# Two heads per score product, no zero products, and norm sums placed inside the chunks of a two-layer block

## Chip, cores, metric

One core of one Trainium2 chip runs the whole program. The metric is device time in microseconds of one execution; three executions of the kernel before and a profiled one are given.

## What is computed

Two layers over 512 positions of width 1024. Each layer has a mixer and a convolutional feed-forward part, both between norms:

```python
h = rms_norm(x, mix_pre_g) * (1 + scale_m) + shift_m
q, k, v, x_lru, gate = split(h @ w_in)               # 512, 128, 128, 512, 512 columns
# chunks of 64 queries see 128 keys; 8 query heads of 64 share 2 key heads; a sink joins the softmax
attn = sliding_window_attention(rope(q), rope(k), v, sinks)
lru = rg_lru(causal_dwconv(x_lru)) * gelu(gate)
y = concat(rms_norm(attn, g_attn), rms_norm(lru, g_lru)) @ w_out
x = x + gate_m * rms_norm(y, mix_post_g)
h = rms_norm(x, ffn_pre_g) * (1 + scale_f) + shift_f
g, val = split(causal_dwconv(h @ w_up))              # 3072 columns each
x = x + gate_f * rms_norm((gelu(g) * val) @ w_down, ffn_post_g)
```

`scale`, `shift` and `gate` are products of silu(c) with `ada_w`, 4 MB for each of twelve vectors. Everything is float32.

## The kernel before

Everything lies transposed: 128 rows of the width on the partitions, positions on the free side, so `x` and `y` are eight tiles of 128x512. Each weight chunk (512 KB, 128 output columns) is split into a high part (ScalarE copy to fp32r, L567) and a low part (VectorE subtraction, L1111); so is each activation (`hH`, `hL`, or `mH`, `mL`). One output tile is 8 x 3 products: high by high, high by low, low by high. A ring of six chunk slots is refilled by SyncE once TensorE has used a chunk. Every engine has its own hand-written order of steps; semaphores tie them.

At a transition a norm must be finished before the next product can start. So the positions are cut in two halves `h` of 256: while TensorE works on half 1 of the last chunks of one matrix, the norm of half 0 goes on, and while it works on half 0 of the next matrix (`next_group`), the norm of half 1 does. `k = 0` is the transition from `w_out` to `w_up`, `k = 1` the one from `w_down` to the `w_in` of the next layer. A norm chain of one half goes so: squares (ScalarE), their sum over tiles (VectorE, `add_square`), the sum over partitions (TensorE, products of one column with `ones`, `post_sums_mm`), root (ScalarE, `post_root`), reciprocal (VectorE, `post_recip`), spread over partitions (TensorE, `post_spread`), residual update (VectorE, `x_update`), squares of the new `x` (`x_squares`), `x_fold`, `x_sums_mm`, `x_root`, `x_recip`, `x_spread`, and then per tile `tmp_half`, `hi_half`, `lo_half` make the operands of the next products.

Two chunks share one PSUM bank of 512 columns, a half each (`pair_bank`). Before their products, `open_bank` writes the bank with a product of zeros (`nil`) that has 512 columns. Scores of a pair of windows (`scores_mm`) are 16 products of 64 rows by 64 stationary columns, for each of 8 heads and of two windows one. During layer 0, VectorE also makes the `ada_w` dot products (`mod_unit`, L1117, called by `late` at the transition), whose weights GpSimd fetches.

## Time and profile before

| | us |
|---|---|
| median of 3 executions | 1204.27 (1202.68 to 1209.97) |
| profiled execution, its own time | 1212.97 |
| span in its trace | 1211.2 |
| TensorE busy | 1176.0 |
| VectorE busy | 833.5 |
| ScalarE busy | 540.4 |
| mean granted TensorE clock | 0.972 |

Busy time is a union of instruction spans. Matmuls overlap in the pipeline, so what one costs is read from start to start, not from its length. An fp32 product shows as two records, an fp32r product as one.

### The profile page before, as it was taken

The numbers are of one execution on the slowest core, as the hardware profiler recorded it, in microseconds if no ns is written. First come the engines' busy times: TensorE is split into PE (matmuls) and PEld (weight loads), VectorE is DVE, ScalarE is ACT, GpSimd is POOL, SyncE is SP. The second block draws the span as 40 slices with busy tenths as digits, with TensorE's granted clock in tenths as the row PEclk, the third lists the DMA queues.
The fourth block names the chain that finished last, engine by engine and source line by source line (L and its number), as shares of the span: only waits on it lengthen the run. The fifth ranks groups of instructions, "written<-read, shape, count | busy, mean of one in ns | idle before, by whom it ended". The sixth has DMA issues, their size and how long they took to land.

```text
span 1211.2 us, 16364 instructions
## 1 busy us (share of the span) xinstructions
PE 1176.0 (97%) x6686; PEld 1024.2 (85%) x6686; DVE 833.5 (69%) x1307; ACT 540.4 (45%) x880; POOL 53.4 (4%) x110
## 2 busy tenths in 40 slices
PE   7999998999999999999999999999999999999995
PEld 6986898988788888888999779998888888888895
DVE  8899858788877777677587874477753565356645
ACT  5387725454224431444348874445532444134430
POOL 4000010001110011000000000000000000000000
PEclk8999888999999999999999999989999999999997
DMA  9833435046784458544113220304233332323312
GB/s 358 338 105 106 157 103 177 7 169 209 229 275 141 141 187 288 178 143 139 53 36 106 70 85 21 105 1 139 89 103 93 98 102 90 105 88 103 92 48 70
DMA packets 44940, 155.81 MB, mean 129 GB/s; under 512 B 5056, under 2 KB 7360, under 8 KB 44864
## 3 DMA queue, kind: packets, MB, share of 16 engines
q1 hardware_dynamic: 34352, 116.48, 29.2%
q0 software_dynamic: 10368, 37.75, 9.4%
q8 instruction: 53, 0.87, 0.3%
q10 hardware_dynamic: 144, 0.52, 0.1%
q14 instruction: 23, 0.19, 0.0%
HBM read 152.64 MB, written 2.10 MB: 128 GB/s over the span
## 4 chain that ended last, share of the span: by engine, by line
PE 80%; DVE 11%; ACT 5%; issue 2%; DMA 2%; SPq 1%; DVEq 0%
PE ps L1841 80%; DVE sb_wL L1111 2%; DVE sb_R L1572 1%; DVE sb_y L1174 1%; DMA sb_raw<-in_w 1%; DMA sb_stage<-in_ada 1%; ACT sb_R L794 1%; DVE sb_R L1700 1%; DVE sb_x L1178 1%; DVE sb_R L1697 1%; ACT sb_wH L567 1%; PE ps L2087 1%; DVE sb_y L1196 1%; ACT sb_sq L673 0%; DVE sb_adaw L1117 0%
## 5 line engine op out<-in xcount | busy, mean ns | idle before, releaser
L1841 PE MATMUL ps<-sb_hH,sb_wH 128*128 128x512 f32 (+1 forms) x1184 | 422.6, 363 | 6.5 <-ACT sb_hH L614 4.0
L1841 PE MATMUL ps<-sb_hH,sb_wL 128*128 128x512 f32 (+1 forms) x1184 | 417.7, 358 | 0.0
L1841 PE MATMUL ps<-sb_hL,sb_wH 128*128 128x512 f32 (+1 forms) x1184 | 394.9, 358 | 2.3 <-DVE sb_hL L1203 2.3
L1841 PEld LDWEIGHTS ps<-sb_hH,sb_wH 128*128 128x128 f32 x1184 | 228.6, 193 | 42.1 <-ACT sb_hH L614 5.4
L1841 PEld LDWEIGHTS ps<-sb_hH,sb_wL 128*128 128x128 f32 x1184 | 228.5, 193 | 31.4
L1841 PEld LDWEIGHTS ps<-sb_hL,sb_wH 128*128 128x128 f32 x1184 | 214.1, 192 | 34.9 <-DVE sb_hL L1203 2.9
L567 ACT ACTIVATE sb_wH<-sb_raw 128x1024 fp32r<-128x1024 f32 x174 | 181.1, 1052 | 129.4 <-DMA sb_raw<-in_w 129.3
L1111 DVE TENSOR_TENSOR sb_wL<-sb_raw,sb_wH 128x1024 fp32r<-128x1024 f32 x174 | 211.4, 1219 | 30.0 <-ACT sb_wH L567 29.8
L1841 PE MATMUL ps<-sb_mH,sb_wH 128*128 128x256 f32 (+1 forms) x608 | 206.4, 340 | 0.6 <-ACT sb_mH L1019 0.6
L1841 PE MATMUL ps<-sb_mL,sb_wH 128*128 128x256 f32 (+1 forms) x608 | 205.0, 337 | 0.0
L1841 PE MATMUL ps<-sb_mH,sb_wL 128*128 128x256 f32 (+1 forms) x608 | 204.9, 337 | 0.0
L1697 DVE SCALAR_TENSOR_TENSOR sb_R<-ps,sb_par,sb_R 128x511 f32<-128x511 f32 x84 | 62.9, 749 | 98.9 <-ACT sb_R L1013 98.9
L1841 PEld LDWEIGHTS ps<-sb_mH,sb_wH 128*128 128x128 f32 x608 | 118.0, 194 | 12.4 <-ACT sb_mH L1019 1.1
L1841 PEld LDWEIGHTS ps<-sb_mL,sb_wH 128*128 128x128 f32 x608 | 117.9, 194 | 12.3 <-DVE sb_mL L1709 0.4
L1841 PEld LDWEIGHTS ps<-sb_mH,sb_wL 128*128 128x128 f32 x608 | 117.7, 194 | 11.1
L1013 ACT ACTIVATE sb_R<-ps,sb_par 128x512 f32<-128x512 f32 x84 | 65.2, 776 | 112.3 <-PE ps L1841 112.3
L1019 ACT ACTIVATE sb_mH<-sb_I 128x512 fp32r<-128x512 f32 x42 | 26.5, 632 | 101.1 <-DVE sb_I L1707 101.1
L1700 DVE SCALAR_TENSOR_TENSOR sb_R<-ps,sb_par,sb_R 128x510 f32<-128x510 f32 x84 | 62.9, 749 | 3.0
L1117 DVE SCALAR_TENSOR_TENSOR sb_adaw<-sb_adaw,sb_csb 128x1024 f32<-128x1024 f32 x44 | 53.4, 1220 | 8.2 <-DMA sb_adaw<-in_ada 8.0
L1709 DVE TENSOR_TENSOR sb_mL<-sb_I,sb_mH 128x512 fp32r<-128x512 f32 x42 | 29.1, 693 | 29.3 <-ACT sb_mH L1019 29.3
L1009 ACT ACTIVATE sb_I<-sb_R 128x512 f32<-128x512 f32 x42 | 26.6, 633 | 50.0 <-DVE sb_R L1700 50.0
L614 ACT ACTIVATE sb_hH<-sb_y,sb_mod 128x256 fp32r<-128x256 f32 x48 | 22.8, 502 | 29.5 <-DVE sb_y L1196 29.4
(229 smaller groups left out, 1154.2 us busy)
## 6 DMA issues: line engine op xcount, KB each, us to landing
sb_raw<-in_w SPq DMA_DIRECT2D x174, 512.0 KB, 3.6
sb_adaw<-in_ada POOLq DMA_DIRECT2D x44, 512.0 KB, 4.8
sb_stage<-in_ada SPq DMA_DIRECT2D x24, 512.0 KB, 14.2
sb_vw<-in_ada POOLq DMA_DIRECT2D x22, 512.0 KB, 4.7
sb_side<-in_w SPq DMA_DIRECT2D x8, 512.0 KB, 5.0
sb_raw<-in_w SPq DMA_DIRECT2D x8, 384.0 KB, 14.8
sb_stage<-in_ada POOLq DMA_DIRECT2D x6, 512.0 KB, 4.6
sb_x<-in_x SPq DMA_DIRECT2D x4, 512.0 KB, 5.8
```

Source lines behind the costliest of these rows:

```text
L567: nc.scalar.activation(high_of(n), raw_of(n), ACT.Copy).then_inc(w_hi, 1)
L614: nc.scalar.activation(hH[:, j, part_of(h)], yt(j)[:, part_of(h)], ACT.Identity, bias=bias[:, j:j + 1], scale=1.0).then_inc(hi_ready, 1)
L794: last = nc.scalar.activation(R[:, c % 4, part_of(h)], pair_bank(h, p)[:, (c % 2) * HALF:(c % 2 + 1) * HALF], ACT.Identity, bias=pcol(l, " ...
L1009: nc.scalar.activation(I[:, p % 2, :], R[:, (c - 1) % 4, :], ACT.Gelu_apprx_tanh).then_inc(f_gelu, 1)
L1013: nc.scalar.activation(R[:, c % 4, :], bank(up_bank(u)), ACT.Identity, bias=par_l[:, COLS["fcb"] + col:COLS["fcb"] + col + 1], scale=pcol( ...
L1019: nc.scalar.activation(mH[:, p, :], I[:, 2 + p % 2, :], ACT.Copy).then_inc(act_hi, 1)
L1111: TT(low_of(n), raw_of(n), high_of(n).bitcast(fp32), ALU.subtract).then_inc(w_lo, 1)
L1117: STT(out=tile, in0=tile, scalar=1.0, in1=csb[:, :], op0=ALU.mult, op1=ALU.mult, accum_out=mod[:, seg, kt:kt + 1]).then_inc(ada_used, 1)
L1697: link(STT(out=buf[:, 1:], in0=acc[:, 0:SEQ - 1], scalar=pcol(l, "fcw", 2 * PAIRS + col), in1=buf[:, 1:], op0=ALU.mult, op1=ALU.add))
L1700: STT(out=buf[:, 2:], in0=acc[:, 0:SEQ - 2], scalar=pcol(l, "fcw", col), in1=buf[:, 2:], op0=ALU.mult, op1=ALU.add).then_inc(f_taps, 1)
L1709: TT(mL[:, p, :], I[:, 2 + p % 2, :], mH[:, p, :].bitcast(fp32), ALU.subtract).then_inc(act_lo, 1)
L1841: return nc.tensor.matmul(out, a, b, start=start, stop=stop, **kw)
```

## The change

Four things are altered.

- Scores: `q` is stored so that two heads of a window lie side by side (`turned`), and `scores_mm` makes 8 products of 64 rows by 128 stationary columns, key head 0 and 1 in turn, each key head in a bank of its own. The rows of a score tile are then two heads of 64 queries instead of two windows.
- Zeros: `open_bank` is gone; the first product into a bank carries the start flag.
- Norms: the last squares of a half are no longer added on VectorE but summed over partitions by products of their own (`post_final`), after the sum of the others (`post_early`); at `k = 0` the epsilon comes in as one product with `ident`, and `post_variance` goes. `x_sums_mm` is split in `x_early` and `x_final`. The gate factor is applied by ScalarE as it copies `y` out of PSUM, one instruction per tile; `x_update` at `k = 0` is then one multiplication of 1024 columns instead of four of 256. The calls stand at new places in every engine's order: at `k = 0` `x_final` and `x_spread` of half 0 stand between the products of the last two chunks of `w_out`.
- Around it: seven slots instead of five hold `ada_w` units at this point (five of them in turn instead of three), and the first chunk after the group of six is split before `pair_base(1, 0)` and `pair_taps(1, 0)` instead of behind them.

```diff
-        ADDS = [6, 5]
+        ADDS = [4, 3]
+        def score_tile(half, kv, two):
+            return kv * AT + half * (AT // 2) + two
+        def two_heads(two, w):
+            first = two * 2 * SEQ + w * P
+            return y[:, first:first + P]
...
                 def out_evict(h, i):
+                    if h == 0 and i == 0:
+                        act.wait_ge(fac_ready, l + 1)
...
-                        square(l, 0, 3 * h + i - 1, pair_bank(h, i))
-                    nc.scalar.activation(y4[:, 2 * i:2 * i + 2, part_of(h)],
-                                         pair_bank(h, i).rearrange("p (j t) -> p j t", j=2),
-                                         ACT.Copy).then_inc(out_copied, 1)
+                        nc.scalar.activation(last_sq[h], pair_bank(h, i), ACT.Square).then_inc(last_ready, 1)
+                    for c in range(2):
+                        j = 2 * i + c
+                        last = nc.scalar.activation(yt(j)[:, part_of(h)],
+                                                    pair_bank(h, i)[:, c * HALF:(c + 1) * HALF],
+                                                    ACT.Copy, scale=fac[:, l, 1, j:j + 1])
+                    last.then_inc(out_copied, 1)
...
                 for p in range(3):
+                    if p == 0:
+                        split_step(ring_next(U0 + 1, SLOTS_W - 1))
                     pair_base(1, p)
                     for c in range(2 * p, 2 * p + 2):
-                        if c:
+                        if c > 1:
                             split_step(ring_next(U0 + c, SLOTS_W - 1))
...
-                for j in range(4 * q, 4 * q + 4):
-                    V.mark(STT(out=yt(j)[:, part_of(h)], in0=yt(j)[:, part_of(h)], scalar=fac[:, l, 2 * k + 1, j:j + 1],
-                               in1=bank(POST_BANK[h])[:, 0:HALF], op0=ALU.mult, op1=ALU.mult))
+                if k == 0:
+                    V.mark(TT(ys, ys, rb.unsqueeze(1).broadcast_to([P, 4, HALF]), ALU.mult))
...
                 U0 = B + FFN0
                 factors(l, 1)
                 late(8, 2)
+                late(10, 1)
                 add_square(l, 0, 0, 0)
-                late(10, 2)
+                late(11, 2)
                 add_square(l, 0, 1, 0)
-                late(12, 1)
-                add_square(l, 0, 2, 0)
                 dve.sem_inc(post_summed, 1)
-                late(13, 1)
-                post_variance(l, 0)
+                late(13, 3)
                 post_recip(l, 0, 0)
                 x_update(l, 0, 0, 0)
                 x_update(l, 0, 0, 1)
+                factors(l, 2)
                 x_fold(l, 0, 0, 0)
                 lo_chunk(U0)
                 x_fold(l, 0, 0, 1)
-                late(14, 2)
...
-            def post_sums_mm(l, k, h):
+            def post_early(l, k, h):
                 pe.wait_ge(post_summed, norm_half(l, k, h))
-                half_sums(h, 0, sum_of[h]).then_inc(post_cols, 1)
+                if k == 0:
+                    part_mm(bank(STAT_BANK[h])[:, 0:2], ident[:, :], eps_a[:, 2 * h:2 * h + 2], True, False)
+                half_sums(h, 0, sum_of[h], k == 1, False)
+                if k == 1:
+                    for t in range(2):
+                        first = h * HALF + t * P
+                        part_mm(bank(STAT_BANK[h])[:, t:t + 1], sum_full[:, first:first + P], ones[:, 0:1],
+                                False, False)
+            def post_final(l, k, h):
+                pe.wait_ge(last_ready, norm_half(l, k, h))
+                half_sums(h, 0, last_sq[h], False, True).then_inc(post_cols, 1)
...
-                    for s in range(NQ):
-                        at_ = HD * (s // AT)
-                        for half in range(2):
-                            w = (2 * t + half) * CHUNK
-                            last = mm(bank(0, 2)[half * CHUNK:(half + 1) * CHUNK, s * P:(s + 1) * P],
-                                      yt(s % AT)[at_:at_ + HD, w:w + CHUNK],
-                                      kd[at_:at_ + HD, w:w + P], True, True)
+                    for half in range(2):
+                        w = (2 * t + half) * CHUNK
+                        for two in range(AT // 2):
+                            for kv in range(NKV):
+                                at_, s = HD * kv, score_tile(half, kv, two)
+                                last = mm(bank(0, 2)[:, s * P:(s + 1) * P],
+                                          two_heads(two, 2 * t + half)[at_:at_ + HD, :],
+                                          kd[at_:at_ + HD, w:w + P], True, True)
...
                 for h in range(2):
+                    if h:
+                        post_early(l, 0, 0)
                     for c in range(GRP):
...
+                        split = KT - 1 if h and c == 1 else AT
+                        if split > AT:
+                            half_products(acc, n, h, mH, mL, range(AT, split), False, False)
+                            post_spread(l, 0, 0)
...
+                        if h and c == 0:
+                            post_final(l, 0, 0)
+                        if h and c == GRP - 1:
+                            x_early(l, 0, 0)
...
-                x_sums_mm(l, 0, 0)
-                x_spread(l, 0, 0)
                 def statistics(k):
...
-                        if at_ == 1:
-                            post_sums_mm(l, k, 1)
-                        if at_ == 3:
+                        if at_ == 0:
+                            post_early(l, k, 1)
+                        if at_ == 2 * KT + GRP + 1:
+                            post_final(l, k, 1)
+                        if at_ == 2 * KT + GRP + 2:
                             post_spread(l, k, 1)
+                        if at_ == (KT + GRP + 4 if k == 0 else KT + 4):
+                            x_early(l, k, 1)
                         if at_ == KT + 4:
-                            x_sums_mm(l, k, 1)
+                            x_final(l, k, 1)
```

## Rows read from the trace of the kernel before

**Rows 1.** Page: busy time by engine, and the granted TensorE clock in 40 slices.
```profile
PE 1176.0 (97%) x6686; PEld 1024.2 (85%) x6686; DVE 833.5 (69%) x1307; ACT 540.4 (45%) x880; POOL 53.4 (4%) x110
...
PEclk8999888999999999999999999989999999999997
```

**Rows 2.** Groups of TensorE instructions by line and form, whole run (count | busy, mean | idle).
```profile
L1841 PE MATMUL ps<-sb_nil 128*128 128x512 f32 x36 | 13.8, 463 | 1.1 <-ACT sb_adaw L742 1.1
```

**Rows 3.** Timeline of TensorE, layer 0, scores of the second window pair (start, length).
```profile
88.47 1.59 PE L1841 MATMUL ps<-sb_kd,sb_y 64*64 64x128 f32 x32
90.00 1.98 PE L1841 MATMUL ps<-sb_xc,sb_gw 128*128 128x512 f32 x4
92.64 1.09 PE L2087 MATMUL ps<-sb_ident,sb_work 128*128 128x128 f32 x8 [0.66 <-DVE sb_work L1331]
```

**Rows 4.** Timeline of TensorE, layer 0, from w_out to w_up, first half.
```profile
185.04 0.95 PE L1841 MATMUL ps<-sb_ones,sb_ssqv 128*128 128x1 f32 x8
...
197.87 1.84 PE L1841 MATMUL ps<-sb_ones,sb_R 128*128 128x1 f32 x16
200.33 0.71 PE L1841 MATMUL ps<-sb_ident,sb_tiny 128*128 128x128 f32 x4 [0.62 <-DVE sb_tiny L1189]
...
204.65 0.58 PE L1841 MATMUL ps<-sb_hH,sb_wH 128*128 128x256 f32 x1 [2.89 <-ACT sb_hH L614]
```

**Rows 5.** Timeline of TensorE, layer 0, second half of the same transition.
```profile
222.59 1.95 PE L1841 MATMUL ps<-sb_ones,sb_R 128*128 128x1 f32 x16 [0.37 <-DVE sb_R L1183]
...
226.67 1.05 PE L1841 MATMUL ps<-sb_ident,sb_tiny 128*128 128x128 f32 x4
...
229.32 0.60 PE L1841 MATMUL ps<-sb_nil 128*128 128x512 f32 x2
229.76 0.28 PE L1841 MATMUL ps<-sb_hH,sb_wH 128*128 128x256 f32 x1
...
249.45 0.50 PE L1841 MATMUL ps<-sb_hH,sb_wH 128*128 128x512 f32 x1 [1.27 <-DVE sb_wL L1111]
```

**Rows 6.** Timeline of TensorE, layer 1, the same three places.
```profile
769.81 0.95 PE L1841 MATMUL ps<-sb_ones,sb_ssqv 128*128 128x1 f32 x8
...
810.25 1.06 PE L1841 MATMUL ps<-sb_ident,sb_tiny 128*128 128x128 f32 x4
...
832.90 0.50 PE L1841 MATMUL ps<-sb_hH,sb_wH 128*128 128x512 f32 x1 [1.13 <-DVE sb_wL L1111]
```

**Rows 7.** Groups of VectorE instructions by form, 166 to 262 us.
```profile
L1111 DVE TENSOR_TENSOR sb_wL<-sb_raw,sb_wH 128x1024 fp32r<-128x1024 f32 x11 | 13.0, 1217 | 0.0
...
L1174 DVE SCALAR_TENSOR_TENSOR sb_y<-sb_y,sb_fac,ps 128x256 f32<-128x256 f32 x16 | 6.6, 476 | 2.1 <-PE ps L1841 2.1
...
L1178 DVE TENSOR_TENSOR sb_x<-sb_x,sb_y 128x1024 f32<-128x1024 f32 x4 | 4.9, 1225 | 0.1
```

**Rows 8.** Groups of ScalarE instructions by form, 166 to 262 us.
```profile
L567 ACT ACTIVATE sb_wH<-sb_raw 128x1024 fp32r<-128x1024 f32 x11 | 11.2, 1050 | 0.0
L614 ACT ACTIVATE sb_hH<-sb_y,sb_mod 128x256 fp32r<-128x256 f32 x16 | 7.7, 502 | 11.1 <-DVE sb_y L1196 11.1
...
L783 ACT ACTIVATE sb_y<-ps 128x512 f32<-128x512 f32 x8 | 4.7, 591 | 0.0
```

**Rows 9.** Stretches at the lower clock: busy time, and the granted clock third from last.
```profile
143.00:160.00 17.00, 17.00 (x79) 16.82 (x79) 6.70 (x14) 4.93 (x11) 1.62 (x4) 0.50 0.31 103
...
224.90:228.30 3.40, 3.40 (x18) 3.40 (x18) 0.67 (x3) 0.02 (x1) 0.00 (x0) 0.51 0.02 5
```

**Rows 10.** Timeline of TensorE from w_down of layer 0 to w_in of layer 1.
```profile
632.35 1.95 PE L1841 MATMUL ps<-sb_ones,sb_R 128*128 128x1 f32 x16 [0.37 <-DVE sb_R L1183]
...
649.41 0.39 PE L1841 MATMUL ps<-sb_hL,sb_wH 128*128 128x256 f32 x1 [0.86 <-DVE sb_hL L1203]
```

**Rows 11.** Timeline of TensorE: end of the first up group, and the tail.
```profile
309.54 0.50 PE L1841 MATMUL ps<-sb_mH,sb_wH 128*128 128x512 f32 x1 [0.63 <-ACT sb_mH L1019]
...
1198.41 1.86 PE L1841 MATMUL ps<-sb_ones,sb_scr 128*128 128x1 f32 x8 [2.75 <-DVEq L1744]
```

More of the change, by code:

```diff
@@ L272, in build @@
         stage_in = [sem(f"stage_in{i}") for i in range(2 * KT)]
-        ada_in = [sem(f"ada_in{i}") for i in range(5)]
+        ada_in = [sem(f"ada_in{i}") for i in range(7)]
         ada_used = sem("ada_used")
@@ L357, in rope_no, with turned @@
             return l * GRP + h * (GRP // 2) + i + 1
+        def score_tile(half, kv, two):
[3 more added lines that the diff above has]
+            return y[:, first:first + P]
+        def turned(j, n, h):
+            first = j // 2 * 2 * SEQ + h * SEQ + j % 2 * CHUNK
+            step = 2 * SEQ - CHUNK if j % 2 else CHUNK
+            if n == 1:
+                rows = y[:, first:first + SEQ].rearrange("p (w m q) -> p w m q", w=4, m=2)
+                return rows[:, :, 0, :]
+            rows = y[:, first:first + n * step].rearrange("p (j r) -> p j r", j=n)[:, :, 0:SEQ]
+            return rows.rearrange("p j (w m q) -> p j w m q", w=4, m=2)[:, :, :, 0, :]
         def in_bank(i):
@@ L403, in build @@
         LATE_UNITS = range(IN_UNITS.stop, DEPTH * NMOD * KT)
+        OUT_UNITS = range(IN_UNITS.stop, 5 * KT)
         def unit_slot(u):
-            return u % 2 if u in IN_UNITS else 2 + u % 3
+            if u in IN_UNITS:
+                return u % 2
+            return 2 + ((u - OUT_UNITS.start) % 5 if u in OUT_UNITS else (u - OUT_UNITS.stop) % 3)
         def unit_fill(u):
@@ L1640, in _ @@
                 lo_half(l, 0, 0, 3)
-                post_variance(l, 1)
                 lo_half(l, 0, 0, 4)
@@ L1947, in next_group @@
                         finish(last, h, c)
+                        between(h, KT + c)
                     for c in range(4, GRP):
@@ L1968, in half_sums @@
                         first = g * HALF + t * P
-                        last = mm(bank(STAT_BANK[h])[:, at_ + t:at_ + t + 1], src[:, first:first + P], ones[:, 0:1],
-                                  g == 0, g == 1)
+                        last = part_mm(bank(STAT_BANK[h])[:, at_ + t:at_ + t + 1], src[:, first:first + P], ones[:, 0:1],
+                                       opens and t == 0 and g == 0, closes and g == 1)
                 return last
@@ L2031, in _ @@
                     mm(pair_bank(h, i), nil[:, :], nil[:, 0:1].broadcast_to([P, SEQ]), True, True)
-            for h in range(2):
-                for i in range(GRP // 2):
-                    open_bank(h, i)
             pe.wait_ge(csb_ready, 1)
@@ L2338, in _ @@
                             pe.wait_ge(dn_read, dn_no(l, GROUPS - 1, 1))
[L2339 to L2349 removed]
+                        acc, n = pair_acc(h, i, c), D0 + c
+                        split = KT // 2 + 1 if h and c == 2 else KT // 2
+                        if h and c == 2:
+                            post_early(l, 1, 0)
+                        half_products(acc, n, h, mH, mL, range(split), True, False)
+                        if h and c == 2:
+                            post_final(l, 1, 0)
+                        if h and c == 6 and l + 1 < DEPTH:
+                            x_early(l, 1, 0)
+                        if h and c == 7 and l + 1 < DEPTH:
+                            x_spread(l, 1, 0)
+                        last = half_products(acc, n, h, mH, mL, range(split, KT), False, True)
+                        finish(last, h, c)
+                        if h and c == 2:
+                            post_spread(l, 1, 0)
+                        if h and c == 6 and l + 1 < DEPTH:
+                            x_final(l, 1, 0)
                 if l + 1 < DEPTH:
@@ L2352, in _ @@
                 else:
-                    post_sums_mm(l, 1, 1)
+                    post_early(l, 1, 1)
+                    post_final(l, 1, 1)
                     post_spread(l, 1, 1)
@@ L2428 @@
     put("fcw", columns(a["ffn_conv_w"].reshape(L, FCONV * 2 * DFF)))
-    put("sink", np.broadcast_to(a["attn_sinks"][:, None, :], (L, P, NQ)))
+    row_head = np.array([[kv * AT + 2 * two + p // CHUNK for kv in range(NKV) for _ in range(2) for two in range(AT // 2)]
+                         for p in range(P)])
+    put("sink", a["attn_sinks"][:, row_head])
     half = HD // 2
```

212 lines of the change are left out of this document (104 added, 108 removed).

## The prediction

> **What bounds the kernel now.** The page comes first: TensorE is busy for 1176.0 of 1211.2 us, at full clock in most slices [rows 1]. So the end is set by TensorE's own work, by its few gaps, and by the stretches in which it is granted half of its 2.4 GHz. The windows show the last: 17 us from 143 on, 3.4 us from 224.9 on, and five more like these [rows 9]. The timeline of TensorE then shows the gaps in the places that the change touches. In layer 0, after the last product of `w_out`, come 16 column sums, 0.62 us idle, the spread, the zero products, and 2.89 us idle until `hH` is there [rows 4]; in the second half 0.37 us idle before the sums and 1.27 us before the first chunk of 512 columns [rows 5]. Each time the clock fell after such a place: TensorE had done 16 one-column sums and waited. Layer 1 repeats the places [rows 6], the transition to `w_in` has two of them [rows 10].
>
> Prices are taken from start to start. Two zero products take 229.76 - 229.32 = 0.44 us, 0.22 each [rows 5]. From 185.04 to 197.87 stand 96 products of 256 columns, eight records of column sums (0.95) and a spread: 12.83 us, so with 0.12 for a product 0.36 are left for the spread [rows 4]. Sixteen records of column sums take 1.84 [rows 4], 0.115 each.
>
> **Scores.** Now 32 records from 88.47 to 90.00 [rows 3], 1.53 us. A record streams 128 columns and still starts 0.048 after the one before, less than half of the 0.109 below, so several run at once; the two windows of a head use different columns of the array, the key heads different rows. After the change there are 16 records in two row groups, each key head's eight in a row. Eight records one after the other take eight times 0.109 (the 0.12 of 256 columns, less a little), 0.9 us with its start about 1.0: a gain of 0.5 per call. If the row groups don't run at once, it is 16 x 0.109 = 1.75, a loss of 0.2. I take the gain, since two groups of columns share the array in the row shown. Of eight calls two stand ahead of 92.64, where TensorE waits 0.66 for `normalise` on VectorE anyway [rows 3]: nothing. Six give 3.0 us. The Trainium skill (TensorEngine Tiling, Theoretical Speedup) lets products that are small both ways run up to four at once, those that are small one way two; by that rule the 32 records would need eight steps before and the 16 need eight after, and nothing would be gained. The row disagrees for before: 1.53 us are 14 steps of 0.109, not eight.
>
> **Zeros.** 36 records of such products of 512 columns are in the trace [rows 2], 30 go. Six at the start lie before a wait; twelve are in `next_group` and counted below. Of twelve in `attn_products` most cost 0.22, those in the 17 us at half clock [rows 9] twice that; two in layer 0 stand ahead of small waits. Together 12 x 0.22 + 0.4 - 0.4 = 2.6 us.
>
> **`w_out` to `w_up`, the main term.** I count from the start of half 1 of `w_out` to the start of the last spread (`x_spread` of half 1). Before: the post sums start two chunks of 12 products (2.88) after it, and the last spread at 226.67, so 226.67 - 185.04 + 2.88 = 44.5 us [rows 4, 5]. Layer 1: 810.25 - 769.81 + 2.88 = 43.3 [rows 6]. After, if TensorE never waits and the clock stays up: 120 + 132 = 252 products x 0.12 = 30.2; column sums in half 0 34 records (two of the epsilon product, 8 + 8, 8 + 8) and in half 1 as many, 68 x 0.115 = 7.8; three spreads 1.1. That is 39.1 us: 5.4 and 4.2 less. The change adds column sums here (20 records, 2.3 us, since what VectorE no longer adds is summed by products) and takes away 3.5 us of gap, 0.9 of zeros, 0.4 of waiting and the two low-clock stretches.
>
> Does TensorE never wait? VectorE and ScalarE have to keep step. From start to start an instruction costs some 0.08 us less than its length on VectorE and 0.1 less on ScalarE; so a low part of a chunk 1.14, a step of 256 columns (`tmp`, `lo`) 0.4 [rows 7], a high part 0.95, `hi` 0.41 [rows 8]. `x_update` was 4 x 0.41 + 1.14; now it is twice the 1.14 of a 1024-column addition, 2.3 instead of 2.8 [rows 7]. An eviction on ScalarE was 2 x 0.49; the copy becomes two of 256 columns at 0.41 to 0.46 [rows 8], so 1.4 instead of 1.0, which is 0.4 more, 16 times, on an engine that is idle half the time here. Counting the new order through from the start of half 1: post spread at 4.6; `x_update` done at 7.6 and 9.9 (layer 0's last three `ada_w` units end at about -0.4, since five slots keep them fetched); second `x_fold` at 12.5, wanted at 13.5; `hi_half` 0 at 17.9, wanted at 19.1; low part of chunk 3 at 18.8, wanted at 19.1; in the next half post reciprocal at 24.1, wanted at 25.0; second fold at 33.9, wanted at 36.8. Everything fits, with margins of 0.3 to 3 us. That is thin: what is late next is VectorE.
>
> Behind the last spread, the chunk of 512 columns started 249.45 - 226.67 = 22.8 us later [rows 5], in layer 1 22.65 [rows 6]. TensorE's own work is 0.36 + 13 x 1.44 = 19.1. The split of that chunk moves ahead of four tap operations, 2.2 us earlier, and `lo_half` 7 ahead of `pair_taps(0, 1)`; so about 20.1, a gain of 2.6. Layer 1 keeps it: 4.2 + 2.6 = 6.8. Layer 0 doesn't: there VectorE, with its `ada_w` units, is behind TensorE for the whole first up group, and TensorE waits for it at 309.54 [rows 11]. What TensorE gains over VectorE is lost there; VectorE's own gain is that of the spread, 5.4 + 0.3 at full clock, less 0.5 for taps that now stand behind the split: 5.2. Price if that were wrong: up to 2.4 more.
>
> **`w_down` to `w_in`.** Half 0 gets 12 more records (8 + 4 + 8 instead of 8), 1.34 us, and so does half 1; two pairs of zeros (0.88), the wait ahead of 632.35 (0.4 shown, 0.8 with the drain) and the low clock behind it (0.8 within the stretch) go; but the wait at 649.41 grows by 0.6, because it is `lo_half` 7 on VectorE that ends it [rows 10]. Sum 2.7 - 0.9 - 0.8 - 0.8 - 0.4 + 0.6, near 0; between -1.5 and +2.
>
> **Tail.** Half 0 of the last layer gets 1.3 us of column sums; the last sums, for which TensorE waits 2.75 us [rows 11], no longer wait for two additions on VectorE of 512 and 256 columns, 1.2 by the prices above: -1.2. Near 0.
>
> **Sum.** -3.0 - 2.6 - 5.2 - 6.8 = -17.6 against 1212.97. The median of the runs is 8.7 us lower than the profiled execution, as if some of the low-clock stretches were not in it (17 us at half clock alone cost up to 8.5 [rows 9]). About 3 us of my sum are such stretches; I take half off. Thin margins and new column sums will cost some stalls; 2 us for them. 1204.3 - 17.6 + 1.5 + 2 = 1190.2.
>
> **Rivals.** (1) The chain on VectorE and ScalarE becomes the bound inside the chunks: the gap moves between products, where TensorE's order makes it wait at `post_final`, `post_spread` or `lo_half`. For it: margins of 0.3 us, 0.4 us more per eviction, VectorE behind in layer 0. Against it: VectorE does 3 us less per layer. Half of the 12 us is lost: 1196.5. (2) The row groups don't overlap: 6 x 0.7 = 4.3 more, 1194.5. (3) The slower side: the clock. Column sums keep TensorE occupied but are not the work that holds its clock up [rows 5, 9]; the change has more of them, and the zero products of 512 columns, which were work to the clock, are gone. If it falls after each of eleven groups of sums, each costs 1.7 us (3.4 at half speed), and if layer 1's attention norm, where it fell for 3.4 us, gets a stretch like the 17 us of layer 0, 7 more: 1190 + 19 + 7 = 1216, slower than before from about eight falls on. Against it: after the change 12 products stand between two groups of eight records, where 16 stood in a row. The Trainium skill has this rule (TensorE: Matmul & The Clock Gate, The HAM clock gate): throttled is the default state and activity releases it; by it removing idle time pays twice, and removing products of zeros can cost. (4) The moved pieces gain only what the zeros and scores do: 1204.3 - 5 = 1199.
>
> **Chances.** Forecast 1190 (own range 1185 to 1195) 0.55; rival 1 0.24; rival 2 0.09; rival 3 0.05; rival 4 0.07. About 1% (12 us) is what a measurement of this kernel can tell from no change; below 1192.2 counts as faster. Nearly all of that lies in the forecast's case, two thirds of it and a deeper tail: faster 0.50, within 1% 0.45, slower 0.05. The range has to reach rival 1 and most of 4, and downward a case where layer 0 keeps its 2.4 and the low-clock stretches weigh in full: 1183 to 1200.
>
> **What would show it.** Scores: 16 records in about 1.0 us; 1.75 is rival 2. Only six records with `nil` and 512 columns. From the first `post_early` of a layer to the last `x_spread` about 39 us, with no idle time over 0.5 us on TensorE and no slice of PEclk below 9 there; idle time ahead of a product that reads `hL`, or of a spread, is rival 1; lower clock behind column sums is rival 3. In layer 0 the wait near 309.54 grows from 0.6 to about 3 us. The first up chunk of 512 columns starts about 20 us after the last spread. The prediction is wrong if layer 0's first up group ends as late as before, or if 17 us at half clock come and go between executions and hide the rest.

## Result and profile after

The changed kernel takes 1198.51 us (median of 11 runs, 1192.47 to 1201.18); the kernel before, run beside it, 1204.27 (11 runs, 1201.89 to 1212.32). The ratio of the two is 0.9941, with a 95% interval of 0.992 to 0.9961. By the ratio the change gives 7.1 us, 0.6%; by the two medians it gives 5.8. The direction is as forecast, but 14.1 us were forecast (1204.3 - 1190.2), so the gain is half of it by the ratio and two fifths by the medians. The two profiled executions are further apart, 1212.97 and 1199.15 us, with spans of 1211.2 and 1197.3.

The page of the changed kernel, busy times and granted clock (before: [rows 1]):

```profile
PE 1165.3 (97%) x6616; PEld 1016.3 (85%) x6616; DVE 821.9 (69%) x1267; ACT 544.4 (45%) x896; POOL 52.1 (4%) x110
...
PEclk8999889999999999999999999999999999999998
```

TensorE lost 10.7 us of busy time. In the clock line each digit stands for 30 us. Only the slices from 120 to 180 us and the two ends are low; the low slices of the transitions before are gone.

Zero products and scores, groups by form and the timeline of TensorE in layer 0 (before: [rows 2, 3]):

```profile
L1869 PE MATMUL ps<-sb_nil 128*128 128x512 f32 x6 | 1.6, 395 | 0.0
```

```profile
110.98 1.16 PE L1869 MATMUL ps<-sb_kd,sb_y 64*128 64x128 f32 x16
112.07 1.09 PE L1869 MATMUL ps<-sb_adaw,sb_vw 128*64 128x256 f32 x8
```

Six zero products are left. The 16 score records take 1.09 us where the 32 took 1.53.

From `w_out` to `w_up` in layer 0, timeline of TensorE (before: [rows 4, 5]):

```profile
180.30 0.28 PE L1994 MATMUL ps<-sb_tiny,sb_ident 128*128 128x2 f32 x2
180.44 1.03 PE L1994 MATMUL ps<-sb_ones,sb_ssqv 128*128 128x1 f32 x8
...
184.81 0.60 PE L1869 MATMUL ps<-sb_ident,sb_tiny 128*128 128x128 f32 x4
...
196.01 0.60 PE L1869 MATMUL ps<-sb_ident,sb_tiny 128*128 128x128 f32 x4
...
219.37 0.60 PE L1869 MATMUL ps<-sb_ident,sb_tiny 128*128 128x128 f32 x4
...
240.31 0.50 PE L1869 MATMUL ps<-sb_hH,sb_wH 128*128 128x512 f32 x1 [1.63 <-DVE sb_wL L1149]
...
248.27 0.50 PE L1869 MATMUL ps<-sb_hH,sb_wH 128*128 128x512 f32 x1 [2.20 <-DVE sb_wL L1149]
```

Within this stretch TensorE no longer waits for a column sum or a spread. The first post sum now stands at the start of half 1 of `w_out`, and from there to the last spread it is 219.37 - 180.30 = 39.1 us, where 44.5 stood. But 20.9 us further on TensorE waits for the low part of the first chunk of 512 columns, and again for the second; layer 1 has the same two waits (1.51 at 815.95, 2.22 at 823.91). In the view of TensorE's waits (total, times, longest) this is now the largest item; it was 2.4 us in two waits before (1.27 of it in [rows 5], 1.13 in [rows 6]):

```profile
PE ps L1869 <- DVE sb_wL L1149: 7.6, 4, 2.2
PE ps L1869 <- DVE sb_tiny L1251: 5.4, 1, 5.4
PE ps L1869 <- DVE sb_ssqv L1269: 3.5, 1, 3.5
PE ps L2129 <- DVE sb_mL L1429: 1.5, 1, 1.5
```

The windows of the changed kernel (length; busy time of TensorE, its weight loads, VectorE, ScalarE, GpSimd; then the granted clock as a share of 2.4 GHz) show where the clock is low (before: [rows 9]):

```profile
138.50:159.00 20.50, 20.35 (x94) 19.23 (x95) 8.73 (x17) 6.15 (x14) 3.14 (x6) 0.50 0.41 145
180.44:221.24 40.80, 40.80 (x349) 40.80 (x348) 28.56 (x44) 21.21 (x39) 0.00 (x0) 1.00 0.27 89
240.31:253.85 13.54, 11.33 (x48) 9.04 (x49) 11.01 (x31) 7.70 (x13) 0.00 (x0) 1.00 0.32 107
824.50:827.90 3.40, 3.40 (x10) 2.62 (x9) 2.40 (x8) 2.54 (x5) 0.00 (x0) 0.51 0.02 8
```

In this trace the transition of layer 0, column sums included, runs at 1.00. The attention half of layer 0's `w_out` has 20.5 us at 0.50, the lower of the two levels (1.2 GHz). In layer 1 another 3.4 us at the lower level follow right behind the second of the two waits, at 824.50.

### The profile page after: what moved, and what is told of

Read it like the earlier page. It is cut to its first block, busy times and chain, and to the rows that moved or that the text cites. A ratio compares the mean times of both kernels' runs of the same rounds, so it can differ in the third digit from the quotient of the medians.

```text
span 1197.3 us, 16181 instructions
## 1 busy us (share of the span) xinstructions
PE 1165.3 (97%) x6616; PEld 1016.3 (85%) x6616; DVE 821.9 (69%) x1267; ACT 544.4 (45%) x896; POOL 52.1 (4%) x110
## 4 chain that ended last, share of the span: by engine, by line
PE 80%; DVE 13%; ACT 4%; issue 2%; DMA 1%; SPq 0%; DVEq 0%
PE ps L1869 57%; PE ps L1894 21%; PE ps L1994 2%; DVE sb_wL L1149 2%; DVE sb_R L1614 1%; DVE sb_stage L1155 1%; ACT sb_R L828 1%; ACT sb_wH L595 1%; DVE sb_R L1736 1%; DVE sb_R L1733 1%; DVE sb_y L1233 1%; ACT sb_sq L700 1%; DVE sb_xc L1381 0%; DVE sb_adaw L1155 0%; DMA sb_raw<-in_w 0%
## 5 line engine op out<-in xcount | busy, mean ns | idle before, releaser
L1869 PE MATMUL ps<-sb_hH,sb_wH 128*128 128x512 f32 x800 | 315.3, 394 | 7.6 <-DVE sb_wL L1149 7.6
L1869 PE MATMUL ps<-sb_hH,sb_wL 128*128 128x512 f32 x800 | 312.1, 390 | 0.0
L1869 PE MATMUL ps<-sb_hL,sb_wH 128*128 128x512 f32 x800 | 311.9, 390 | 0.0
L1149 DVE TENSOR_TENSOR sb_wL<-sb_raw,sb_wH 128x1024 fp32r<-128x1024 f32 x174 | 211.7, 1219 | 30.3 <-ACT sb_wH L595 30.1
L1869 PE MATMUL ps<-sb_mH,sb_wH 128*128 128x512 f32 x288 | 112.1, 389 | 0.9 <-ACT sb_mH L1055 0.9
L1869 PE MATMUL ps<-sb_mL,sb_wH 128*128 128x512 f32 x288 | 112.2, 389 | 0.0
L1869 PE MATMUL ps<-sb_mH,sb_wL 128*128 128x512 f32 x288 | 112.1, 389 | 0.0
L1894 PE MATMUL ps<-sb_hH,sb_wH 128*128 128x256 f32 x384 | 104.3, 290 | 0.1
L1894 PE MATMUL ps<-sb_hH,sb_wL 128*128 128x256 f32 x384 | 102.9, 287 | 0.0
L1894 PE MATMUL ps<-sb_mH,sb_wH 128*128 128x256 f32 x320 | 94.6, 296 | 0.2 <-ACT sb_adaw L769 0.2
L1894 PE MATMUL ps<-sb_mL,sb_wH 128*128 128x256 f32 x320 | 92.4, 289 | 0.0
```

Of the source, the lines that this page charges most:

```text
L1149: TT(low_of(n), raw_of(n), high_of(n).bitcast(fp32), ALU.subtract).then_inc(w_lo, 1)
L1869: return nc.tensor.matmul(out, a, b, start=start, stop=stop, **kw)
L1894: return nc.tensor.matmul(out, a, b, start=start, stop=stop, skip_group_check=True)
```

## Where the time went: a ledger by stages

Each stage runs from the first product of one kind to the first of the next, so that the same stage of the program stands in each row (us). P is what the prediction gave the stage. The last three columns come from experiments 8 and 7 below: the two kernels with twelve products of zeros added in the stage of the second row, layer 0, which held the clock there.

| stage | before | after | diff. | P | before, clock held | after, clock held | diff. |
|---|---|---|---|---|---|---|---|
| start to layer 0's `w_out` | 131.65 | 128.04 | -3.6 | -1.0 | 132.91 | 127.89 | -5.0 |
| attention half of `w_out`, to the spread | 30.14 | 32.02 | +1.9 | -1.3 | 24.19 | 23.77 | -0.4 |
| from there to the end of the first up group | 147.75 | 143.11 | -4.6 | -5.2 | 147.75 | 144.65 | -3.1 |
| up and down groups, transition to `w_in` | 350.01 | 349.57 | -0.4 | 0 | 349.38 | 351.07 | +1.7 |
| layer 1: `w_in`, scores | 63.09 | 61.61 | -1.5 | -2.0 | 63.09 | 61.61 | -1.5 |
| attention half of `w_out` | 23.92 | 21.55 | -2.4 | -1.3 | 22.40 | 21.55 | -0.9 |
| from there to the end of the first up group | 145.67 | 143.46 | -2.2 | -6.8 | 145.61 | 141.87 | -3.7 |
| the rest | 318.93 | 317.98 | -1.0 | 0 | 317.61 | 317.48 | -0.1 |
| span | 1211.2 | 1197.3 | -13.8 | -17.6 | 1202.9 | 1189.9 | -13.1 |

The second row went against the forecast by 3.2 us, and the seventh, layer 1's transition, fell short by 4.6. The trace of the changed kernel with zeros has 3.4 us at the lower clock in the third and in the fourth row which the changed kernel's own trace doesn't have; they cost 1.5 us each. It lacks the 3.4 us at 824.50 in the seventh, where it is 1.6 us shorter.

The clock enters this ledger in two places, and the traces of all kernels together show both (numbers in brackets are those of the experiments). "Wait" is TensorE's wait ahead of the transposition of layer 0's last probabilities, which lies in the stage of the second row. "Low in stage" is the time at the lower clock in that stage, and "low elsewhere" the same for the rest of the program, without the first 30 us and the last 20.

| trace | scores | norms | wait | stage | low in stage | low elsewhere |
|---|---|---|---|---|---|---|
| before, first | old | old | 0.28 | 30.1 | 17 | 27 |
| before, again (1) | old | old | none | 24.7 | 6 | 20 |
| norms alone (3) | old | new | none | 24.6 | 6 | 7 |
| zeros alone (4) | old | old | 0.71 | 21.9 | 0 | 24 |
| scores alone (5) | new | old | 1.10 | 30.9 | 17 | 24 |
| scores and zeros (2) | new | old | 1.54 | 32.1 | 21 | 20 |
| changed | new | new | 1.53 | 32.0 | 21 | 3 |
| changed, split back (9) | new | new | 1.54 | 28.7 | 14 | 10 |
| changed, base ahead (10) | new | new | 1.53 | 32.0 | 21 | 3 |
| changed, attention zeros back (6) | new | new | 1.10 | 24.7 | 3 | 7 |
| changed, twelve zeros (7) | new | new | 0.21 | 23.8 | 0 | 7 |
| the same and base ahead (11) | new | new | 0.22 | 23.8 | 0 | 3 |
| the same and second split (12) | new | new | 0.22 | 23.8 | 0 | 3 |
| before, twelve zeros (8) | old | old | none | 24.2 | 0 | 20 |

The column on the right goes by the norms: 20 to 27 us at the lower clock with the old ones, 3 to 10 with the new. The column beside it goes more by the scores: with the new ones and no zeros added or put back it is 14 to 21 us in all five traces, and with the old ones and no zeros added it is 17, 6, 6 and 0. The wait alone doesn't decide it, since the first trace has 17 us behind a wait of 0.28.

## Experiments

All times are medians, with the ratio to runs of the kernel before on the same chip and its 95% interval. The experiments were run on three chips, on which the kernel before has medians of 1203.46 to 1204.50 us. Each run also has its mean granted clock. The runs of one kernel lie near a line, 8 to 11 us for 0.01 of clock where the clock varies much; "at 0.982" is the value of that line. It compares kernels at the same mean clock and says nothing of where the low clock lies; where no run of a kernel reached 0.982, as in experiments 2 and 5, it is an estimate from outside its runs.

**1. The kernel before again.** No edit.

> The kernel before, unchanged, for the granted clock of each of its runs. Eleven runs of the changed kernel lie on one line: 1192.47 us at a granted clock of 0.990, 1196.7 to 1198.5 at 0.984, 1201.2 at 0.980, so 8.7 us for 0.01 of clock. Theory A: the profiled execution of the kernel before (1212.97 us at 0.972) carried low-clock stretches that most of its executions lack; on the same slope 1204.3 us lies at 0.982, and at equal clock the two kernels are 5 to 7 us apart, half of the 13.8 us between the two profiled executions. Theory B: at equal clock they are 10 us or more apart, and the change itself lowers the clock (stretch of 20.5 us at half clock in layer 0); then most runs of before show a clock of 0.986 or more at 1204 us.

1205.00 us, ratio 1.001 (0.998 to 1.004); clocks 0.972 to 0.986, median 0.980. In the 35 runs of the kernel before beside it the same: 1199.84 to 1213.14 us, median 0.980, 1202.7 us at 0.982. The changed kernel has 1198.9 at 0.982 and a median clock of 0.984. So neither theory quite: 3.8 us at equal clock, and over the whole program the change raises the mean clock rather than lowering it. The profiled execution of the kernel before, at 0.972, was at the low end of its runs. The second trace has, in the attention half of layer 0's `w_out`:

```profile
133.34:158.02 24.68, 24.35 (x181) 23.59 (x180) 17.69 (x34) 14.76 (x24) 2.09 (x4) 0.87 0.29 102
```

24.7 us at a mean clock of 0.87, where the first trace had 30.1. This stage is 5.5 of the 6.8 us between the two.

**2. and 3. The two halves of the change.** In one kernel scores and zeros as after and the norms as before, in the other the reverse: the hunks of `turned`, `score_tile`, `two_heads`, `scores_mm`, `outputs_mm` and the sinks, and those of the zeros, of which the core is

```diff
-                    if c % 2 == 0:
-                        open_bank(h, c // 2)
-                    half_products(pair_acc(h, c // 2, c), O0 + c, h, mH, mL, range(AT), False, False)
+                    half_products(pair_acc(h, c // 2, c), O0 + c, h, mH, mL, range(AT), c % 2 == 0, False)
```

> The kernel before with the new scores and without the zero products, norms as before. Prediction's own terms: scores 3.0 and zeros 2.6 us (zeros of the transitions 1.8 more, as far as they are not ahead of a wait), so 1198 us. Theory A: most of this lies ahead of waits or behind a longer low-clock stretch in layer 0's attention norm (the trace of the changed kernel is only 0.8 us ahead when w_out's second half starts); 1201 to 1203. Rival 4 (only these two gain anything): 1198 to 1199, and the run with the norms alone is at 1204.

1204.76 us, ratio 1.0002 (0.9977 to 1.0026). Above what either theory said: no gain, at clocks of 0.969 to 0.976 where before has 0.972 to 0.986. At 0.982 the line gives 1198.7, 4.1 less. By this estimate the clock took back what the products gave.

> The changed kernel with the scores of before and with the zero products put back: the norm chains inside the chunks, the seven slots and the earlier split alone. Prediction: 12 us less than before in work and short low-clock stretches, so 1193 us. Theory A: 4 us in layer 0 and 3 in layer 1, some of it short low-clock stretches that most runs of before lack: 1199 to 1201. Rival 4: 1204, no gain.

1201.08 us, ratio 0.9975 (0.9949 to 1.0), clock 0.986. Between the prediction and nothing, as theory A had it. At 0.982 its line gives 1205.7 us, 3.0 more than the kernel before. So the norms' gain shows as a higher clock (0.986 at the median for 0.980), in line with the 7 us at the lower clock where the old norms have 20 to 27; at equal clock they cost time. By their ratios the two halves alone add up to 2.8 us, and together they give 7.1. Each of these ratios is uncertain by some 3 us, so it isn't shown that the halves depend on each other.

**4. and 5. Zeros alone, scores alone,** on the kernel before: the same hunks, each group by itself.

> The kernel before without its zero products, nothing else. Scores and zeros together gave no time (1204.8) at a median clock of 0.974 instead of 0.980, and 4.1 us less at equal clock. Theory Z (the zeros carry the clock): this run shows clocks of 0.972 to 0.976 and 1203 to 1206 us. Theory S (the shorter scores do): clocks as before, 0.980, and 1201 to 1202.

1201.39 us, ratio 0.9985 (0.996 to 1.0011). Seven runs at 1199.6 to 1201.4 us and 0.979 to 0.982, five at 1208.4 to 1208.9 and 0.972 to 0.974. The traced execution is one of the seven and has no low clock in the attention half of layer 0; that the other five have the stretch there is inferred from their clock, as no trace of them was kept. The median clock stays at 0.980 and the median time is in theory S's range, so the zeros alone don't carry the clock.

> The kernel before with the new scores, zeros kept. 16 records take 1.09 us instead of 1.53, so eight calls give up to 3.5 us of work. Theory Z: clocks as before and 1200.5 to 1202. Theory S: clocks of 0.972 to 0.976 and 1203 to 1206. Phase (neither alone, the clock falls by where the small steps happen to lie): something between, and different in each.

1205.14 us, ratio 1.0003 (0.9982 to 1.0024), clocks 0.975 to 0.980 in all twelve runs. The shorter scores alone gain nothing and never have the good executions of the kernel before. Theory S is nearer. A likely reason stands where layer 0's last probabilities are transposed. Timelines of TensorE: the changed kernel, scores alone, norms alone (where scores are as before):

```profile
136.47 1.06 PE L2129 MATMUL ps<-sb_ident,sb_adaw 128*128 128x128 f32 x8 [1.53 <-DVE sb_mL L1429]
137.37 0.95 PE L1869 MATMUL ps<-sb_ones,sb_sq 128*128 128x1 f32 x8
138.65 1.98 PE L1869 MATMUL ps<-sb_adaw,sb_vw 128*64 128x256 f32 x8 [0.33 <-ACT sb_adaw L779]
140.56 1.87 PE L1869 MATMUL ps<-sb_ones,sb_I 128*128 128x1 f32 x8
```

```profile
136.13 1.06 PE L2112 MATMUL ps<-sb_ident,sb_adaw 128*128 128x128 f32 x8 [1.10 <-DVE sb_mL L1411]
```

```profile
139.36 1.04 PE L2109 MATMUL ps<-sb_ident,sb_adaw 128*128 128x128 f32 x8
```

With the scores of before TensorE is here at 139.4 and doesn't wait (0.28 us in the first trace of the kernel before). With the new ones it starts 3 us earlier and waits 1.1 us, with the zeros gone too 1.5, for VectorE's softmax and low parts. What it gained ahead of this place partly ends in the wait. Behind the wait come only transpositions, column sums and small outputs, and from 138.50 on the clock is 0.50 for 20.5 us. The Trainium skill (TensorE: Matmul & The Clock Gate, HAM oscillation) tells of a kernel whose TensorE waits for transfers between its groups of products and is throttled again each time. Here the wait is for VectorE and short, 1.53 us. The trace agrees in the order only, a wait and then the fall, and the small products around the wait didn't prevent it. The wait is not the whole cause: the first trace of the kernel before fell at the same place with 0.28 us.

**6. Zeros of the attention products put back** into the changed kernel, the diff above read backwards.

> The changed kernel with the twelve zero products of the attention half of w_out put back alone (0.22 us each at full clock, 2.6 in all, some behind waits). Ledger by stages so far: from w_out's first product to the end of the attention columns of half 1, layer 0 takes 30.1 us (17 at half clock) or 24.7 (6) in two traces of the kernel before, 24.6 (6) with zeros and new norms, 32.0 (20) in both traces with the zeros gone. Theory C (the zeros were work to the clock: without them it stays low longer here): the stage takes 25 to 30 us again, granted clocks of 0.984 to 0.990, time 1195 to 1198. Theory W (zeros are only work): 2 to 2.6 us slower than the changed kernel, 1200.5 to 1201.

1200.60 us, ratio 0.9948 (0.9922 to 0.9975). Four runs at 1195.3 to 1196.0 and 0.986 to 0.988, eight at 1199.4 to 1203.1 and 0.981 to 0.984. Theory W has the median, theory C the good third: three zeros per half cost their time, and don't reliably hold the clock. Theory C in this form falls. The traced execution, 1196.02 us, is one of the four; its stage takes 24.7 us with 3.5 at the lower clock.

**7. Zeros put into the wait.** Twelve products of 512 columns, added to an open bank (they change no result), in layer 0 alone:

```diff
                     attn_products(0, 3)
+                    add_zeros(6)
                     probs_transposed(3)
                     attn_cols(2)
+                    add_zeros(2)
                     outputs_mm(3)
+                    add_zeros(2)
                     lru_cols(0)
+                    add_zeros(2)
                     attn_cols(3)
```

> The changed kernel with twelve products of zeros of 512 columns added into an open bank of layer 0's w_out: six ahead of the transposition for which TensorE waits 1.53 us, two each ahead of the three small steps behind it. Theory C: TensorE keeps its clock through the stage, which takes 23 to 25 us instead of 32, no or only one short low-clock stretch there, granted clocks 0.986 to 0.992, time 1190 to 1193. Theory W: 6 of the 12 (1.3 us) are hidden by the wait, the others cost 1.3 us: 1200.

1191.77 us, ratio 0.9883 (0.9847 to 0.9918), six runs within 1.6 us, clocks 0.989 and 0.990. The stage in its windows, and the wait in its timeline:

```profile
127.89:151.65 23.76, 23.55 (x188) 22.10 (x189) 19.08 (x34) 15.58 (x24) 3.14 (x6) 1.00 0.47 169
```

```profile
136.31 1.06 PE L2129 MATMUL ps<-sb_ident,sb_adaw 128*128 128x128 f32 x8 [0.21 <-DVE sb_mL L1429]
```

The transposition starts when it did (8.4 us into the stage, in both), so all of the 8.3 us gained in this stage (32.0 - 23.8) lies behind it, where the clock is 1.00 now. Against the changed kernel's median it is 6.7 us, 7.0 by the ratios. What in the twelve products does it, that they stream or that they fill the wait, isn't told apart: six of them stand in the wait, six behind it.

**8. The same zeros in the kernel before.**

> The kernel before with the same twelve added zero products in layer 0 as in the run that had them on the changed kernel (1191.8 us, all six runs within 1.6 us). It takes the variable stretch of layer 0 out of the comparison of the two kernels. Theory A: the kernel before has it in part of its executions only (the stage takes 24.7 or 30.1 us in its two traces), so it gains less than the changed kernel: 1198 to 1201, and the change with both covered is worth 7 to 9 us. If the 13.8 us between the two profiled executions were the change's own: 1205.

1204.43 us, ratio 0.9996 (0.9974 to 1.0017), all runs from 1202.2 to 1205.9. The stage takes 24.2 us at clock 1.00. So the kernel before gains nothing on average: it loses its bad executions (1209 and more) and, to the cost of twelve zeros, its good ones (1200). Theory A expected a smaller difference between the two kernels: with this stage held in both it is 1204.43 - 1191.77 = 12.7 us, 13.1 by the spans of the traces. The two ran on different chips; by their ratios, each to the kernel before beside it, it is 1.1%, 13.6 us.

This is not all work saved. First, the zeros cost the kernel before more, because it has no wait to put them in; its timeline of TensorE:

```profile
139.76 1.47 PE L1841 MATMUL ps<-sb_nil 128*128 128x512 f32 x6
141.07 1.03 PE L2087 MATMUL ps<-sb_ident,sb_adaw 128*128 128x128 f32 x8
```

Six zeros take 141.07 - 139.76 = 1.3 us here, and nothing in the changed kernel, where they fill the wait. Second, the windows of this trace still have the short stretches at the lower clock in and around the transitions. Four of its five are:

```profile
197.20:204.00 6.80, 4.04 (x19) 4.04 (x20) 6.62 (x14) 3.06 (x7) 0.00 (x0) 0.50 0.08 31
221.00:224.40 3.40, 3.40 (x19) 3.40 (x18) 1.13 (x3) 0.80 (x2) 0.00 (x0) 0.50 0.03 5
780.80:784.20 3.40, 2.81 (x13) 2.81 (x14) 3.25 (x7) 2.78 (x6) 0.00 (x0) 0.50 0.02 5
801.20:804.60 3.40, 3.40 (x18) 3.40 (x18) 0.29 (x2) 0.20 (x1) 0.00 (x0) 0.51 0.00 0
```

That is 20 us at the lower clock where the changed kernel with zeros has 7. At the 1.5 us that 3.4 us of it cost in the ledger, the difference is an estimated 6 us. So of the 12.7 us about 1.3 are the zeros' own cost and about 6 are the clock of the transitions; some 5 are left for work and waits.

**9. The earlier split taken back**, on VectorE and likewise on ScalarE:

```diff
                 for p in range(3):
-                    if p == 0:
-                        lo_chunk(ring_next(U0 + 1, SLOTS_W - 1))
                     pair_taps(1, p)
                     for c in range(2 * p, 2 * p + 2):
-                        if c > 1:
+                        if c:
```

> The changed kernel with the split of the first chunk behind the group of six put back behind four tap operations. In its trace TensorE now waits 1.6 and 2.2 us (layer 0) and 1.5 and 2.2 us (layer 1) for low parts of the first and the second chunk of 512 columns. Theory V (VectorE's chain of taps, products and splits is the bound behind the last spread): the first chunk starts some 1 to 2 us later after the spread, the wait ahead of the second shrinks below 1.2 us, and the kernel is 0 to 2 us faster than the changed one, 1196.5 to 1198.5. Prediction's step (TensorE is the bound there, the earlier split is a gain of 2.6 us in layer 1): 1200 to 1203.

1199.75 us, ratio 0.9946 (0.9925 to 0.9968), not to be told from the changed kernel. TensorE's waits for low parts in its timeline:

```profile
239.50 0.50 PE L1865 MATMUL ps<-sb_hH,sb_wH 128*128 128x512 f32 x1 [3.80 <-DVE sb_wL L1147]
```

```profile
816.47 0.50 PE L1865 MATMUL ps<-sb_hH,sb_wH 128*128 128x512 f32 x1 [3.69 <-DVE sb_wL L1147]
```

3.80 us once instead of 1.63 + 2.20. Neither of the two ranges was met. With the split put back the whole wait stands ahead of the first chunk of 512 columns, and there is none ahead of the second. The earlier split only moves it from one chunk to the next and takes nothing off it, so VectorE's chain is the bound there.

**10. The next pair's base ahead of this pair's gelu** on ScalarE, for the pairs (0, 2) and (1, 0) to (1, 2), in the changed kernel. What it aims at is the timeline of VectorE between the two waits of layer 1 (changed kernel); each step waits half a microsecond for ScalarE, which in turn waits for VectorE:

```profile
818.60 0.43 DVE L1629 TENSOR_TENSOR sb_I<-sb_I,sb_R 128x256 f32<-128x256 f32 x1 [0.48 <-ACT sb_I L836]
819.51 0.42 DVE L1638 TENSOR_TENSOR sb_mL<-sb_I,sb_mH 128x256 fp32r<-128x256 f32 x1 [0.48 <-ACT sb_mH L842]
820.42 0.22 DVE L1612 SCALAR_TENSOR_TENSOR sb_R<-sb_edge,sb_par,sb_R 128x1 f32<-128x1 f32 x1 [0.49 <-ACT sb_R L828]
...
822.64 2.35 DVE L1149 TENSOR_TENSOR sb_wL<-sb_raw,sb_wH 128x1024 fp32r<-128x1024 f32 x2
```

```diff
-                    pair_base(1, p)
+                    if p < 2:
+                        pair_base(1, p + 1)
...
                     pair_gelu(1, p)
```

> The changed kernel with one reordering on ScalarE behind the last spread: the first tap product of a pair (pair_base) of the next pair stands ahead of the gelu of this one, so that VectorE finds it ready. TensorE now waits 1.6 and 2.2 us (layer 0), 1.5 and 2.2 (layer 1) for the low parts of the first two chunks of 512 columns. Theory V (the round trip between ScalarE and VectorE per pair, not the amount of work on either, sets these): some 0.9 us less per pair, the four waits fall from 7.6 to under 2 us, time 1192 to 1195. Rival (the waits are set by VectorE's own work or by when TensorE closes the pairs): waits as before, 1198 to 1199.

1192.86 us, ratio 0.9885 (0.9843 to 0.9927), six runs over clocks of 0.982 to 0.990; 1195.8 at 0.982, 3.1 less than the changed kernel. The waits:

```profile
PE ps L1871 <- DVE sb_wL L1151: 5.3, 4, 1.6
```

From 7.6 to 5.3, not under 2: a third of the waits is this round trip (the idle time ahead of the taps). How the rest divides between VectorE's own work and the two other trips of each pair wasn't tested. Of the 5.6 us between the medians only about 3 are this edit by the line at 0.982; three of the six runs had clocks of 0.987 to 0.990.

**11. and 12. Both, and a further step.** Experiments 7 and 10 together; then also the second chunk's split ahead of the taps of pair (1, 1), on VectorE and likewise on ScalarE:

```diff
-                        if c > 1:
+                        if c > 2:
                             lo_chunk(ring_next(U0 + c, SLOTS_W - 1))
                     pair_product(1, p)
                     pair_low(1, p)
+                    if p == 0:
+                        lo_chunk(ring_next(U0 + 2, SLOTS_W - 1))
```

> Both edits together. Theories C and V: the two gains add, 1184 to 1189. If either falls, this lies beside the other one alone.

1188.16 us, ratio 0.9854 (0.9815 to 0.9893): 3.6 less than with the zeros alone, at the same clocks of 0.989 to 0.991. So the two add up as expected.

> The run with both edits (1188.2 us) and the split of the second chunk behind the group of six moved ahead of the taps of pair (1, 1) on both engines. In that run TensorE still waits 1.0 us ahead of the first and 1.6 us ahead of the second chunk of 512 columns, in both layers. Theory V: the second wait falls below 0.5 us, nothing else becomes late: 1185 to 1187. Rival: the third chunk's low part is late instead, 1188.

1187.83 us, ratio 0.9852 (0.9821 to 0.9882), no difference that can be told from the kernel of experiment 11. The view of waits says why half of it is missing:

```profile
PE ps L1875 <- ACT sb_mH L1059: 2.5, 1, 2.5
PE ps L1875 <- DVE sb_wL L1153: 2.0, 2, 1.1
```

The second wait is gone in both layers, as theory V said. Something else did become late, but not the third chunk of the rival: in layer 0, 2.5 us of waiting stand at the end of the first up group, at the place of [rows 11]. There ScalarE itself waits 2.4 us for VectorE (`sb_I`), which has `ada_w` units between its taps.

## Why the prediction was right in direction and wrong in size

The prediction gave 1190.2 us as its forecast and missed by 8.3; it counted a time below 1192.2 as faster, so this result falls into its case "within 1%". What each part of it said, and what the runs showed:

- **Scores.** Predicted 1.0 us for 16 records and 0.5 gained per call; measured 1.09, 0.44 in layer 0 and 1.48 / 4 = 0.37 in layer 1. Rival 2 is out. The 0.4 us gained also disagree with the equal number of steps that the prediction drew from the Trainium skill (TensorEngine Tiling, Theoretical Speedup). The step that gave the calls of layer 0 their full worth failed: they bring TensorE early to a wait on VectorE (experiment 5). Against this stands that the stage ahead of `w_out` gained 3.6 to 5.0 us where 1.0 was in the sum. The wait at its end shrank from 1.09 us to 0.22; the rest isn't traced, and the stage's length differs by 1.7 us between two traces of the kernel before (131.65, 133.34).
- **Zeros.** Predicted 2.6 us for both layers. In layer 1's attention half, with no low clock in either trace with zeros added, it is 0.9 where 1.3 were given. The run without them has a median 2 to 3 us lower, but its interval includes no change.
- **`w_out` to `w_up`.** The main count held: 39.1 us from first post sum to last spread in layer 0, 39.1 in layer 1 (756.06 to 795.13), with no idle time and at full clock in the trace of the changed kernel; the first chunk of 512 columns starts 20.9 and 20.8 us behind the spread (20.1 predicted). In layer 0 the term is -4.6 for -5.2, and what TensorE gained was lost again to VectorE as forecast, though at the second chunk, not at 309.54.
- **The step that failed in the sum** is "a gain of 2.6. Layer 1 keeps it: 4.2 + 2.6 = 6.8": measured 2.2, and 3.7 with no low clock. From the start of this stage to the first chunk of 512 columns layer 1 does gain 6.3 us (86.3 before, 80.1 after); at the second chunk 3.9 are left and at the third, behind the 3.4 us of low clock, 2.2. I followed the chain to the first chunk of 512 columns and stopped; the second one's low part stands behind eight more tap operations and came 2.22 us late. Rival 1 named this mechanism, but looked for it between the products of the transition. Experiments 9 and 10 show it.
- **The larger step that failed** is the clock. I took the 17 us at half clock in layer 0 as a matter of the execution that the change leaves alone, and set the whole sum against the median with 1.5 us for the clock. The traces show that the change makes it more frequent: all five traces with the new scores and no zeros added or put back have 14 to 21 us of it, those with the old scores and no zeros added 17, 6, 6 and 0. By the mean clocks nearly all runs of the changed kernel have it in whole or in part (ten of eleven at 0.980 to 0.985, one at 0.990 and 1192.47 us). Held away by zeros, the changed kernel is 6.7 us faster. Rival 3 had the engine and the direction, but put the low clock behind the column sums of the transitions and into layer 1's attention norm. The prediction's last sign of being wrong, that the 17 us come and go between executions and hide the rest, is what happened.
- **The term that was right by luck.** With the stage held in both kernels the difference is 12.7 us, close to the 14.1 forecast, but not made up as forecast. "About 3 us of my sum are such stretches" undercounts the short low-clock stretches of the transitions: 20 us of them against 7 in the two traces, some 6 us of time by the estimate of experiment 8. Work and waits outside the clock gave less than the sum had. The column sums of the transitions, though there are more of them, had a clock of 1.00 in the changed kernel's trace; the trace with zeros has one stretch of 3.4 us in layer 0's transition (195.4 to 198.8).
- **`w_down` to `w_in`, tail.** Forecast near 0 each. The stages that contain them changed by -0.4 and -1.0 between the profiled executions. Twelve records at the prediction's 0.115 are 1.38 us, not 1.34, which changes nothing in its sum.

What stays open: why the stretch comes in some executions of one and the same kernel and not in others. The traces show only that it starts at this place. With twelve zeros there it was in none of the four traces of kernels that had them, and the run times of each of these kernels lie within 1.4 to 3.6 us.

## What to carry over

A gain on the bounding engine counts up to the next place where it waits for somebody else; follow the order of work to the second and third such place, not to the first. When a median and a profiled execution differ, list the stages at the lower clock in more than one trace first: a stage whose length varies between executions of one kernel is part of the cost, and a change that moves an engine's arrival can come with it more often, as here. Twelve products of zeros at that place, half of them inside the wait, gave 6.7 us here.

## Unexpected of the hardware

- With twelve products of zeros, six of them in a wait of 1.5 us, TensorE kept its full clock through a stage of 24 us; without them it ran 20.5 us of that stage at 0.50. The run times then spread over 1.5 us (six runs) instead of 8.7 (eleven runs).
- The granted clock was low for 20 to 27 us outside this stage in the six traces with the old norms, and for 3 to 10 in the eight with the new ones, although these have more column sums.
- 16 score products of 64 rows by 128 stationary columns in two row groups start 0.068 us apart (1.09 / 16), 32 of 64 by 64 did so 0.048 apart: half the products gave 29% less time, not half.
